# Two gate_up pieces of the first expert pair fetched outside the ring of weight slots

## The chip, the cores and the metric

One NeuronCore of one Trainium2 chip. The time is that of one execution on the device in microseconds, the median of three runs.

## The reference

One layer of a streaming encoder in float32. 272 prompt rows (16 meta tokens and 256 others) and 8 x 16 sample rows go through an RMS norm, an input projection, two kinds of attention (8 heads with a forget bias, 4 differential heads), an output projection and a residual. Then a mixture of 32 experts, four for each row, is added. The mixture's weights are what this case is about:

```python
D_MODEL = 1024; N_EXPERTS = 32; TOP_K = 4; D_FF = D_MODEL
SWIGLU_LIMIT = 7.0; SWIGLU_ALPHA = 1.702
...
def ffn(h, l):
    return h + _moe(_rms(h, ffn_norm[l]), w_router[l], b_router[l], w_gate_up[l], b_gate_up[l],
                    w_down[l], b_down[l])
```

Each expert has w_gate_up (1024 x 2048), a clamped SwiGLU, and w_down (1024 x 1024). Every expert is computed, so 32 x 12.6 MB of weights are read, 403 MB in all, whatever the routing is.

## The kernel before

All of SBUF is one tensor, `arena`, cut by hand into regions that stages share one after the other. Each engine has a program of its own, and semaphores order them. The attention half fills about the first 250 us. Then come the output projection in six steps (`project_out`, line 1752, each counted by `o_done` and added to `y` by VectorE), the router for three tiles of rows (`logits`, `route`; counted by `logit_done`, and by `gates_ready` when the last gates are written), and a first gather of rows (`gather_first`, line 1824).

The mixture runs over 16 **pairs** of experts. For each pair the host layout gives 12 **pieces** of 128 x 4096 float32 (2 MiB, one DMA each, issued by SP): pieces 0 to 7 are gate_up (two experts in turn, four quarters of 256 weight rows each), pieces 8 to 11 are down. Counted through all pairs they are pieces 0 to 191. They lie in a **ring** of 8 slots (`RING`); piece q stands in slot (q + 2) % 8. SP's `refill` waits until TensorE has finished piece j (`piece_done`) and then issues piece j + 8 into the same slot. TensorE's `pair` (line 1881 gate_up, line 1916 down) waits for two pieces at a time: pieces 0 and 1 at the pair's start, 2 and 3, 4 and 5, 6 and 7 at steps k = 2, 4, 6, then 8 and 9, 10 and 11. After a pair's gate_up it gathers the next pair's rows (line 1856), transposes the activations (1898), multiplies by down, and scatters the rows back (1931).

Pieces of the first pair can't be fetched as soon as their slots exist, since the slots hold attention data and output weights at first. Before the loop SP issues pieces 1, 3 and 2 (line 534), then, when attention is over, the router's weights and pieces 4 and 5 (line 538). Pieces 6 and 7 go to slots 0 and 1, where the output projection's weights lie until its last step: SP waits for `o_done` 6, issues six small bias loads (lines 541 and 543), then pieces 6 and 7 (line 545). Piece 8 waits for piece 0 to be done (line 553, in a hardware loop over pairs two at a time).

In the last pair TensorE runs some products into an unused bank (`keep_busy`, line 1742), which are idle filling.

Of the kernel before, what the change touches and what calls it, by code (L numbers as in the profile page):

```python
# [12 lines left out]
D = 1024  # L13
# [19 lines left out]
PAIRS = E // 2  # L33
# [3 lines left out]
SLOT_W = 2048  # L37
PIECE_W = 4096
LEAD = 2
Y_BASE = 6  # L40
X_ORDER = (1, 2, 3, 0)
X_BANK = (6, 2, 6, 0)
# [48 lines left out]
def build(nc, io, out):  # L91
    ctx = ExitStack()
    with ctx:
# [5 lines left out]
        def sem(name):  # L99
            return ctx.enter_context(nc.semaphore(name))  # L100

        def at(off, n):
            return arena[:, off:off + n]
# [92 lines left out]
        gT = at(a0 + 13312, 384)  # L196
        sel = [at3(a0 + 13696 + 768 * i, 3, P) for i in range(2)]
        selg = [at3(a0 + 13696 + 768 * i + 384, 3, P) for i in range(2)]
        rt = at(a0 + 11264, 512)
        EQ = [at3(a0 + 12288 + P * t, E, TOPK) for t in range(3)]  # L200
        EG = at3(a0 + 12288 + 3 * P, E, TOPK)
        bgu4 = at(hn0, 512)
# [12 lines left out]
        ovo = at(hn0 + 3008, 80)  # L215
        ovm = at(hn0 + 3088, 16)
        junk2 = act

        ident = C["ident"]

# [10 lines left out]
        s_x = [sem(f"s_x{t}") for t in range(4)]  # L231
        s_win = [sem(f"s_win{b}") for b in range(6)]
        s_wout = sem("s_wout")
        ring_in = [sem(f"ring_in{i}") for i in range(RING)]
        s_ck, s_cv = [sem("s_ck0"), sem("s_ck1")], [sem("s_cv0"), sem("s_cv1")]
        s_v3 = [sem("s_v3_0"), sem("s_v3_1")]
# [148 lines left out]

        block = ctx.enter_context(nc.Block())

        def run_pairs(eng, body):

            with eng.Fori(0, PAIRS // 2 - 1) as it:
                for u in range(2):
                    body(it, u, lambda k, c, u=u: it * (2 * k) + (u * k + c),
                         lambda k, c, u=u: it * (2 * k) + ((u + 1) * k + c))
            it = PAIRS // 2 - 1
            for u in range(2):
                body(it, u, lambda k, c, u=u: (2 * it + u) * k + c,
                     (lambda k, c, u=u: (2 * it + u + 1) * k + c) if u == 0 else None)
# [18 lines left out]
        def _(sp):  # L417
# [116 lines left out]
                sp.dma_start(piece_slot(s), piece_src(0, s - LEAD)).then_inc(ring_in[s], 16)  # L534
            sp.wait_ge(mixed, NA)
            sp.dma_start(w_rt, io["w_router"][0].rearrange("(k p) e -> p k e", p=P)).then_inc(s_wrt, 16)
            for n_ in (4, 5):
                sp.dma_start(piece_slot(n_ + LEAD), piece_src(0, n_)).then_inc(ring_in[n_ + LEAD], 16)
            sp.wait_ge(o_done, 6)
            for n in range(4):  # L540
                sp.dma_start(bgu4[E * n:E * (n + 1)], io["b_gate_up"][0, :, 512 * n:512 * (n + 1)]).then_inc(s_bgu, 16)
            for hf in range(2):
                sp.dma_start(bdn2[E * hf:E * (hf + 1)], io["b_down"][0, :, 512 * hf:512 * (hf + 1)]).then_inc(s_bdn, 16)
            for n_ in (6, 7):
                sp.dma_start(piece_slot(n_ + LEAD - RING), piece_src(0, n_)).then_inc(ring_in[n_ + LEAD - RING], 16)

            def refill(it, j):

# [3 lines left out]
                s = (q + LEAD) % RING  # L552
                sp.dma_start(piece_slot(s), piece_src(pair, q % PIECES)).then_inc(ring_in[s], 16)

            with sp.Fori(0, PAIRS // 2 - 1) as it:
                for j in range(2 * PIECES):
                    refill(it, j)
            for j in range(2 * PIECES - RING):
# [906 lines left out]
        def _(pe):  # L1465
# [378 lines left out]
            gather_first(1, (4, 5, 6, 7))  # L1844
            gather_first(2, range(8))
            totals()
            pe.wait_ge(s_bgu, 64)
            pe.wait_ge(s_bdn, 32)

            def gather(at_, u):
# [9 lines left out]
            def pair(at_, u, arrived, next_at=None, last_one=False):  # L1861
                steps = [(k, n) for k in range(6) for n in range(4)] + [(k, n) for n in range(4) for k in (6, 7)]
                for k, n in steps:
                    if (k, n) == (0, 0):
                        pe.wait_ge(xg_a, at_(4, 1))
                    if (k, n) == (1, 0):
                        pe.wait_ge(own_ready, at_(1, 1))
                        for n_ in range(4):
                            grp = slice(E * n_, E * (n_ + 1))
                            mm(banks[n_], own_e[u][grp], bgu4[grp], start=False, stop=False, skip_group_check=True)  # L1870
                        pe.wait_ge(xg_a, at_(4, 4))
                    if (k, n) == (4, 0):
                        pe.wait_ge(xg_v, at_(1, 1))
                    if (k, n) == (6, 0) and last_one:
                        keep_busy(banks[7], 512, 2)
                    if k % 2 == 0 and n == 0:
                        s = [arrived(k + x) for x in range(2)]
                    for x in range(2):
                        half = slice(SLOTS * x, SLOTS * (x + 1))
                        c0 = 2 * FF * (k % 2) + 512 * n  # L1880
                        last = mm(banks[n][half], XT[u][:, k, half], piece_slot(s[x])[:, c0:c0 + 512],  # L1881
                                  start=(k == 0), stop=(k == 7), skip_group_check=True)
                        if n == 3 and k % 2 == 1:
                            last.then_inc(piece_done, 1)
                    if n < 3 and k == 7:
                        last.then_inc(h_done, 1)
                if next_at:
                    gather(next_at, 1 - u)
                pe.wait_ge(act_ready, at_(4, 2))
                for hf in range(2):  # L1890
                    grp = slice(E * hf, E * (hf + 1))
                    mm(banks[hf], own_e[u][grp], bdn2[grp], start=True, stop=False, skip_group_check=True)  # L1892
                if last_one:
                    keep_busy(banks[7], 512)
                pe.wait_ge(y_added, at_(6, Y_BASE))
                pe.wait_ge(act_ready, at_(4, 4))
                for c in range(8):
                    last = nc.tensor.transpose(banks[4 + c // 4][:, P * (c % 4):P * (c % 4 + 1)],  # L1898
                                               act[:, P * c:P * (c + 1)], ident)
                    if c % 4 == 3:  # L1900
                        last.then_inc(actT_done, 1)
                pe.wait_ge(selg_ready, at_(1, 1))
                for t in range(3):
                    last = nc.tensor.transpose(banks[3][:, P * t:P * (t + 1)], selg[u][:, t], ident)
                last.then_inc(selT_done, 1)
                pe.wait_ge(actT_a, at_(1, 1))
                for i in range(2):
                    if i == 1:
                        pe.wait_ge(actT_v, at_(1, 1))
                    s = [arrived(8 + 2 * i + x) for x in range(2)]  # L1910
                    for hf in range(2):
                        for c in range(4):
                            for x in range(2):
                                half = slice(SLOTS * x, SLOTS * (x + 1))
                                w = piece_slot(s[x])[:, D * c + 512 * hf:D * c + 512 * (hf + 1)]
                                last = mm(banks[hf][half], actT[:, 4 * i + c, half], w, start=False,  # L1916
                                          stop=(i == 1 and c == 3), skip_group_check=True)
                                if c == 3 and hf == 1:
                                    last.then_inc(piece_done, 1)
                        if i == 1 and hf == 0:  # L1920
                            last.then_inc(down_done, 1)
                pe.wait_ge(selT_copied, at_(1, 1))
                for n in range(6):
                    t, hf = n // 2, n % 2
                    if n == 0:
                        pe.wait_ge(rows_a, at_(1, 1))
                    elif n == 1:
                        pe.wait_ge(rows_v, at_(1, 1))
                    else:
                        pe.wait_ge(y_added, at_(6, Y_BASE + n - 1))  # L1930
                    mm(banks[4 + n % 2], gT[:, P * t:P * (t + 1)], rows[:, 512 * hf:512 * hf + 512],  # L1931
                       start=True, stop=True).then_inc(scat_done, 1)

            def main(it, u, at_, nx):
                def arrived(r):
                    q = PIECES * u + r
                    s = (q + LEAD) % RING
                    pe.wait_ge(ring_in[s], it * (16 * 3) + 16 * (q // RING + 1))
                    return s
                pair(at_, u, arrived, nx, nx is None)  # L1940

            run_pairs(pe, main)

            def over(p, r_, at_):
                def arrived(r):
                    s, uses, use = over_slot(r)
                    before_ = 16 * PAIRS * PIECES // RING
                    pe.wait_ge(ring_in[s], at_(16 * uses, before_ + 16 * (use + 1) - PAIRS * 16 * uses))
                    return s
                pe.wait_ge(y_added, at_(6, Y_BASE))  # L1950
                gather(at_, 0)
                pair(at_, 0, arrived)
# [33 lines left out]
```

## Time and profile before

| | us |
|---|---|
| median of 3 runs | 1246.28 (1246.19 to 1246.39) |
| the profiled execution, whole | 1244.19 |
| its span in the trace | 1242.40 |
| TensorE matmul busy | 1211.3 (97%) |
| TensorE weight loads busy | 530.0 (43%) |
| VectorE, ScalarE, GpSimd busy | 349.7, 194.6, 158.6 |
| DMA: 448.59 MB moved | mean 361 GB/s |

Matmul busy time overlaps itself and counts pipelining, so it is not a distance from the peak. The page's second part cuts the span into 40 slices of 31 us; a digit 9 is a share of 90% or more. Times below are counted from the span's start.

### The profile page before, as it was taken

The page shows a single profiled execution, that of the slowest core. Times are in us where ns is not written, and L with a number is a line of the kernel's source. Part 1 is how long each engine was busy: PE and PEld are TensorE (multiplying, and loading weights), DVE is VectorE, ACT ScalarE, POOL GpSimd, SP SyncE. Part 2 cuts the span into 40 slices and gives each one's busy share as a digit, 9 for nine tenths or more (in the row PEclk, how much of TensorE's full clock was granted, in tenths as well). Part 3 has the DMA queues.
Part 4 walks back from the last instruction along what each step waited for, and adds up shares of the span by engine and source line. Part 5 has one row for each costly group of instructions (what it writes and reads, how often), then busy time and mean ns, then how long its engine had stood idle before and what let it go on. Part 6 is the DMA issues. An engine that isn't in the chain of part 4 may idle for free.

```text
span 1242.4 us, 16212 instructions
## 1 busy us (share of the span) xinstructions
PE 1211.3 (97%) x6099; PEld 530.0 (43%) x6100; DVE 349.7 (28%) x929; ACT 194.6 (16%) x519; POOL 158.6 (13%) x378
## 2 busy tenths in 40 slices
PE   9999999999999999999999999999999999999997
PEld 5444456646344343434343443434343434243432
DVE  3234366613322121213131322212121212131312
ACT  4211365513101010101010100001010101010100
POOL 0032312101320202112020202020202011020000
PEclk9999999999999999999999999999999999999999
DMA  9622344792899999999999999999999999999994
GB/s 299 256 71 93 146 131 148 276 394 72 367 428 428 428 429 427 428 429 429 427 428 429 429 427 427 429 430 428 428 428 429 429 427 428 429 429 427 427 427 198
DMA packets 55450, 448.59 MB, mean 361 GB/s; under 512 B 10465, under 2 KB 11890, under 8 KB 30834
## 3 DMA queue, kind: packets, MB, share of 16 engines
q1 hardware_dynamic: 55368, 448.05, 87.1%
q8 instruction: 25, 0.41, 0.1%
q14 instruction: 15, 0.12, 0.0%
q10 hardware_dynamic: 42, 0.01, 0.0%
HBM read 442.00 MB, written 4.86 MB: 360 GB/s over the span
## 4 chain that ended last, share of the span: by engine, by line
PE 71%; DMA 25%; DVE 1%; issue 1%; SPq 1%; ACT 0%; POOL 0%; DVEq 0%; POOLq 0%
DMA arena<-in_w_gate_up 23%; PE psum L1881 18%; PE psum L1916 17%; PE psum L1627 10%; PE psum L1856 7%; PE psum L1752 3%; PE psum L1931 3%; DMA arena<-in_w_down 2%; PE psum L1892 1%; PE psum L1898 1%; PE psum L1663 1%; PE psum L1731 1%; PE psum L1586 1%; PE psum L1577 1%; PE psum L1602 1%
## 5 line engine op out<-in xcount | busy, mean ns | idle before, releaser
L1881 PE MATMUL psum<-arena 128*64 128x512 f32 x2048 | 454.0, 600 | 15.8 <-DMA arena<-in_w_gate_up 15.8
L1881 PEld LDWEIGHTS psum<-arena 128*64 128x64 f32 x2048 | 148.8, 138 | 316.2 <-issue 316.2
L1916 PE MATMUL psum<-arena 128*64 128x512 f32 x1024 | 223.5, 594 | 0.9
L1426 DVE TENSOR_SCALAR arena<-psum 128x256 f32<-128x256 f32 x64 | 26.8, 419 | 397.3 <-PE psum L1881 397.3
L1916 PEld LDWEIGHTS psum<-arena 128*64 128x64 f32 x1024 | 78.7, 137 | 134.8 <-issue 133.3
L1627 PE MATMUL psum<-arena 128*128 128x512 f32 x288 | 127.3, 596 | 1.4 <-DVE arena L1065 1.4
L1002 ACT ACTIVATE arena<-arena 128x256 f32<-128x256 f32 x64 | 26.7, 418 | 594.8 <-DVE arena L1426 594.8
L1931 PE MATMUL psum<-arena 128*128 128x512 f32 x192 | 93.2, 622 | 0.0
L700 POOL COPY arena<-arena 128x6 f32 (+1 forms) x16 | 3.0, 188 | 698.2 <-PE psum L1916 695.1
L1856 PEld LDWEIGHTS psum<-arena 128*128 128x128 f32 x720 | 81.5, 192 | 12.2 <-issue 12.2
L1856 PE MATMUL psum<-arena 128*128 128x128 f32 x720 | 84.4, 277 | 0.0
L1627 PEld LDWEIGHTS psum<-arena 128*128 128x128 f32 x288 | 53.5, 190 | 64.4 <-issue 62.4
L1444 DVE TENSOR_TENSOR arena<-psum,arena 128x512 f32<-128x512 f32 x96 | 66.4, 692 | 25.3 <-PE psum L1931 25.3
L1439 DVE COPY arena<-psum 128x512 f32<-128x512 f32 x16 | 11.1, 692 | 218.3 <-PE psum L1916 218.3
L1931 PEld LDWEIGHTS psum<-arena 128*128 128x128 f32 x192 | 28.6, 188 | 64.3 <-DVE arena L1444 42.1
L717 POOL TENSOR_SCALAR arena<-arena 128x64 f32<-128x64 f32 x96 | 53.9, 579 | 0.0
L1752 PE MATMUL psum<-arena 128*128 128x512 f32 x96 | 43.1, 597 | 1.0 <-DVE arena L1313 1.0
L1414 DVE TENSOR_TENSOR arena<-arena 128x256 f32<-128x256 f32 x64 | 36.4, 610 | 5.4
L708 POOL TENSOR_SCALAR arena<-arena 128x64 f32<-128x64 f32 x90 | 37.4, 441 | 0.0
L1010 ACT ACTIVATE arena<-psum 128x512 f32<-128x512 f32 x16 | 9.6, 598 | 161.1 <-PE psum L1916 161.1
L1399 DVE TENSOR_SCALAR arena<-psum,arena 128x128 f32<-128x128 f32 x64 | 18.0, 345 | 48.1 <-PE psum L1856 45.8
L1428 DVE SCALAR_TENSOR_TENSOR arena<-arena 128x256 f32<-128x256 f32 x64 | 27.3, 426 | 2.2
(257 smaller groups left out, 795.0 us busy)
## 6 DMA issues: line engine op xcount, KB each, us to landing
arena<-in_w_gate_up SPq DMA_DIRECT2D x128, 2048.0 KB, 25.0
arena<-in_w_down SPq DMA_DIRECT2D x64, 2048.0 KB, 22.1
arena<-in_w_in SPq DMA_DIRECT2D x5, 2048.0 KB, 14.1
arena<-in_cache_fox_k SPq DMA_DIRECT2D x8, 512.0 KB, 3.6
arena<-in_cache_diff_k SPq DMA_DIRECT2D x8, 512.0 KB, 4.5
arena<-in_cache_fox_v SPq DMA_DIRECT2D x8, 512.0 KB, 4.7
arena<-in_cache_diff_v SPq DMA_DIRECT2D x8, 512.0 KB, 5.8
arena<-in_w_out SPq DMA_DIRECT2D x4, 1024.0 KB, 6.7
```

Of the source, the lines that this page charges most:

```text
L708: last = nc.gpsimd.tensor_scalar(sel[u][:, t, cols], places, pRK[u][:, t, x:x + 1], None, ALU.is_equal)
L717: last = nc.gpsimd.tensor_scalar(selg[u][:, t, cols], places, pRK[u][:, t, x:x + 1], pG[u][:, t, x:x + 1], ALU.is_equal, ALU.mult)
L1414: nc.vector.tensor_tensor(act_rows[:, 32 * n:32 * (n + 1)], ta[n % 2].rearrange("s (p q) -> s p q", q=8), sg[n % 2].rearrange("s (p q) -> ...
L1426: nc.vector.tensor_scalar(tg[n % 2], H[:, 0:512:2], 7.0, None, ALU.min).then_inc(glu_ready, 1)
L1428: lk(nc.vector.scalar_tensor_tensor(out=ta[n % 2], in0=tl[n % 2], scalar=1.0, in1=tg[n % 2], op0=ALU.add, op1=ALU.mult))
L1444: nc.vector.tensor_tensor(y[:, t, cols], banks[4 + n % 2], y[:, t, cols], ALU.add).then_inc(y_added, 1)
L1627: last = mm(z_bank(u), hnT[:, k, r0:r0 + n], wv[:, k], start=(k == 0), stop=(k == 7))
L1752: last = mm(banks[4 + n % 2], oT[:, k, P * t:P * (t + 1)], wv[:, k % 2, 512 * hf:512 * hf + 512], start=(k == 0), stop=(k == 7))
L1856: last = mm(banks[6 + k // 4][:, P * (k % 4):P * (k % 4 + 1)], x2n[:, t, P * k:P * (k + 1)], sel[u][:, t], start=(t == 0), stop=(t == 2))
L1881: last = mm(banks[n][half], XT[u][:, k, half], piece_slot(s[x])[:, c0:c0 + 512], start=(k == 0), stop=(k == 7), skip_group_check=True)
L1916: last = mm(banks[hf][half], actT[:, 4 * i + c, half], w, start=False, stop=(i == 1 and c == 3), skip_group_check=True)
L1931: mm(banks[4 + n % 2], gT[:, P * t:P * (t + 1)], rows[:, 512 * hf:512 * hf + 512], start=True, stop=True).then_inc(scat_done, 1)
```

## The change

Pieces 4 and 5 of the first pair leave the ring. Their ring slots (6 and 7) are filled at once with pieces 0 and 1 of the second pair (pieces 12 and 13). Piece 5 goes whole into the region of the activation buffers (`whole_piece`), once the second tile's logits and the last square are done. Piece 4 goes in four runs of columns (1024, 1024, 1280 and 768) into regions that are dead after the routing, once the third tile's logits, the first gather and the gates are done. The loads before the loop are put in another order: piece 6 right after `o_done` 6, then the gate_up biases, piece 5, piece 7, the down biases, piece 4. TensorE waits for the biases where it uses them. On TensorE the first two pairs are written out ahead of the hardware loop, and piece 4's product is cut where a run ends inside a block of 512 columns. SP leaves out the two refills. A small routing buffer (`rt`) moves.

```diff
+APART = (4, 5)
+APART_SLOTS = [(q + LEAD) % RING for q in APART]
...
-        rt = at(a0 + 11264, 512)
+        rt = at(a0 + 12800, 512)
...
+        whole_piece = at(a0 + 8192, PIECE_W)
+        runs = [(0, a0 + 7168, 1024), (1024, a0 + 12288, 1024), (2048, hn0 + 1024, 1280), (3328, a0 + 13312, 768)]
...
+        def run_pairs(eng, body, first_apart=False):
+            if first_apart:
+                for u in range(2):
+                    body(0, u, lambda k, c, u=u: u * k + c, lambda k, c, u=u: (u + 1) * k + c)
+            with eng.Fori(1 if first_apart else 0, PAIRS // 2 - 1) as it:
...
-            for n_ in (4, 5):
-                sp.dma_start(piece_slot(n_ + LEAD), piece_src(0, n_)).then_inc(ring_in[n_ + LEAD], 16)
+            for q, s in zip(APART, APART_SLOTS):
+                sp.dma_start(piece_slot(s), piece_src(1, q + RING - PIECES)).then_inc(ring_in[s], 16)
             sp.wait_ge(o_done, 6)
+            sp.dma_start(piece_slot(6 + LEAD - RING), piece_src(0, 6)).then_inc(ring_in[6 + LEAD - RING], 16)
             for n in range(4):
                 sp.dma_start(bgu4[E * n:E * (n + 1)], io["b_gate_up"][0, :, 512 * n:512 * (n + 1)]).then_inc(s_bgu, 16)
+            sp.wait_ge(logit_done, 2)
+            sp.wait_ge(h_sq, 4)
+            sp.dma_start(whole_piece, piece_src(0, APART[1])).then_inc(s_apart[1], 16)
+            sp.dma_start(piece_slot(7 + LEAD - RING), piece_src(0, 7)).then_inc(ring_in[7 + LEAD - RING], 16)
             for hf in range(2):
                 sp.dma_start(bdn2[E * hf:E * (hf + 1)], io["b_down"][0, :, 512 * hf:512 * (hf + 1)]).then_inc(s_bdn, 16)
-            for n_ in (6, 7):
-                sp.dma_start(piece_slot(n_ + LEAD - RING), piece_src(0, n_)).then_inc(ring_in[n_ + LEAD - RING], 16)
+            sp.wait_ge(logit_done, 3)
+            sp.wait_ge(xg_done, 2)
+            sp.wait_ge(gates_ready, 1)
+            for p0, where, n in runs:
+                sp.dma_start(at(where, n), piece_src(0, APART[0])[:, p0:p0 + n]).then_inc(s_apart[0], 16)
...
-            with sp.Fori(0, PAIRS // 2 - 1) as it:
+            for j in range(2 * PIECES):
+                if j not in APART:
+                    refill(0, j)
+            with sp.Fori(1, PAIRS // 2 - 1) as it:
...
-            pe.wait_ge(s_bgu, 64)
-            pe.wait_ge(s_bdn, 32)
...
+                        pe.wait_ge(s_bgu, 64)
...
-                        last = mm(banks[n][half], XT[u][:, k, half], piece_slot(s[x])[:, c0:c0 + 512],
-                                  start=(k == 0), stop=(k == 7), skip_group_check=True)
+                        for o, w in s[x](c0):
+                            last = mm(banks[n][half, o:o + w.shape[1]], XT[u][:, k, half], w,
+                                      start=(k == 0), stop=(k == 7), skip_group_check=True)
...
+                pe.wait_ge(s_bdn, 32)
...
+                    if isinstance(it, int) and it == 0 and q in APART:
+                        i = APART.index(q)
+                        pe.wait_ge(s_apart[i], 16 * (len(runs), 1)[i])
+                        return (run_parts, piece_parts(whole_piece))[i]
+                    pe.wait_ge(ring_in[s], it * (16 * 3) + (16 * (q // RING + 1) - fewer(s)))
...
-            run_pairs(pe, main)
+            run_pairs(pe, main, first_apart=True)
```

## Rows read from the trace of the kernel before

**Rows 1.** The page, parts 1 and 2: TensorE's busy time; DMA share in 40 slices.

```profile
PE 1211.3 (97%) x6099; PEld 530.0 (43%) x6100; DVE 349.7 (28%) x929; ACT 194.6 (16%) x519; POOL 158.6 (13%) x378
...
DMA  9622344792899999999999999999999999999994
```

**Rows 2.** Waits of TensorE, whole run: total us, times, longest.

```profile
PE psum L1881 <- DMA arena<-in_w_gate_up: 15.8, 10, 2.1
```

**Rows 3.** Windows, second and eighth pair: us, engines' busy time, PE clock, DMA share, GB/s.

```profile
367.30:423.80 56.50, 56.50 (x278) 22.57 (x277) 13.30 (x28) 5.78 (x12) 6.74 (x17) 1.00 1.01 429
...
734.20:792.90 58.70, 56.68 (x275) 22.84 (x275) 13.31 (x28) 5.79 (x12) 6.75 (x17) 1.00 1.01 429
```

**Rows 4.** The chain that ended last, in order of time: start, us, what.

```profile
315.44 24.18 PE psum L1881 x112
...
675.49 8.75 PE psum L1881 x32
...
734.22 7.09 PE psum L1881 x32
...
1197.23 26.34 DMA arena<-in_w_down
1223.57 0.14 issue
1223.71 7.09 PE psum L1916 x32
```

**Rows 5.** DMA issues near 305.0, 319.2, 326.6, 332.9, 375.8 us: last column, us to landing.

```profile
arena<-in_w_gate_up SPq DMA_DIRECT2D x1, 2048.0 KB, 8.0
...
arena<-in_w_down SPq DMA_DIRECT2D x1, 2048.0 KB, 7.2
...
arena<-in_w_down SPq DMA_DIRECT2D x1, 2048.0 KB, 14.5
...
arena<-in_w_gate_up SPq DMA_DIRECT2D x1, 2048.0 KB, 14.6
...
arena<-in_w_down SPq DMA_DIRECT2D x1, 2048.0 KB, 10.7
```

**Rows 6.** Timeline of SP's queue: start, us for all issues of the row, line, count.

```profile
302.30 1.72 SPq L541 DMA_DIRECT2D arena<-in_b_gate_up  x4
...
304.98 0.90 SPq L545 DMA_DIRECT2D arena<-in_w_gate_up  x2
319.22 0.99 SPq L553 DMA_DIRECT2D arena<-in_w_down  x2
...
332.94 0.33 SPq L553 DMA_DIRECT2D arena<-in_w_gate_up  x1
...
375.79 0.91 SPq L553 DMA_DIRECT2D arena<-in_w_down  x2
```

**Rows 7.** Windows before and in the first pair; the last two columns are DMA's.

```profile
290.00:300.00 10.00, 10.00 (x45) 5.95 (x43) 4.77 (x19) 3.65 (x8) 0.00 (x0) 1.00 0.01 2
...
317.00:318.00 1.00, 1.00 (x7) 0.29 (x5) 0.00 (x0) 0.00 (x0) 0.91 (x5) 1.00 0.00 0
```

**Rows 8.** DMA queues, stretches 345:346, 320:424, then 424:1120 (two rows): packets, MB, share.

```profile
q8 instruction: 1, 0.02, 6.6%
...
q8 instruction: 3, 0.05, 0.2%
...
q1 hardware_dynamic: 20478, 298.26, 100.7%
q14 instruction: 1, 0.01, 0.0%
```

**Rows 9.** Timeline before and in the first pair: last gather, last gate copy.

```profile
307.62 3.02 PE L1824 MATMUL psum<-arena 128*128 128x128 f32 x24
...
312.89 0.15 DVE L1449 COPY arena<-arena 128x1 f32<-128x1 f32 x1
```

**Rows 10.** Window inside the 8.75 us stretch of the chain; PE clock before the DMA columns.

```profile
675.50:678.80 3.30, 3.30 (x8) 1.08 (x10) 0.00 (x0) 0.00 (x0) 0.00 (x0) 0.50 1.04 442
```

More of the change, by code:

```diff
@@ L217, in build, with run_parts, piece_parts @@
         junk2 = act
+        whole_piece = at(a0 + 8192, PIECE_W)
+        runs = [(0, a0 + 7168, 1024), (1024, a0 + 12288, 1024), (2048, hn0 + 1024, 1280), (3328, a0 + 13312, 768)]
+        def run_parts(c0):
+            return [(max(p0, c0) - c0, at(where + max(p0, c0) - p0, min(p0 + n, c0 + 512) - max(p0, c0)))
+                    for p0, where, n in runs if p0 < c0 + 512 and p0 + n > c0]
+        def piece_parts(piece):
+            return lambda c0: [(0, piece[:, c0:c0 + 512])]
         ident = C["ident"]
@@ L233, in build @@
         s_wout = sem("s_wout")
+        s_apart = [sem("s_apart0"), sem("s_apart1")]
         ring_in = [sem(f"ring_in{i}") for i in range(RING)]
@@ L386, in build, with fewer @@
         block = ctx.enter_context(nc.Block())
-        def run_pairs(eng, body):
-            with eng.Fori(0, PAIRS // 2 - 1) as it:
+        def fewer(s):
+            return 16 if s in APART_SLOTS else 0
+        def run_pairs(eng, body, first_apart=False):
[3 more added lines that the diff above has]
+            with eng.Fori(1 if first_apart else 0, PAIRS // 2 - 1) as it:
                 for u in range(2):
@@ L1914, in pair @@
                                 half = slice(SLOTS * x, SLOTS * (x + 1))
-                                w = piece_slot(s[x])[:, D * c + 512 * hf:D * c + 512 * (hf + 1)]
+                                w = s[x](D * c + 512 * hf)[0][1]
                                 last = mm(banks[hf][half], actT[:, 4 * i + c, half], w, start=False,
@@ L1937, in arrived @@
                     s = (q + LEAD) % RING
-                    pe.wait_ge(ring_in[s], it * (16 * 3) + 16 * (q // RING + 1))
-                    return s
+                    if isinstance(it, int) and it == 0 and q in APART:
[3 more added lines that the diff above has]
+                    pe.wait_ge(ring_in[s], it * (16 * 3) + (16 * (q // RING + 1) - fewer(s)))
+                    return piece_parts(piece_slot(s))
                 pair(at_, u, arrived, nx, nx is None)
-            run_pairs(pe, main)
+            run_pairs(pe, main, first_apart=True)
             def over(p, r_, at_):
@@ L1947, in arrived @@
                     before_ = 16 * PAIRS * PIECES // RING
-                    pe.wait_ge(ring_in[s], at_(16 * uses, before_ + 16 * (use + 1) - PAIRS * 16 * uses))
-                    return s
+                    pe.wait_ge(ring_in[s], at_(16 * uses, before_ + 16 * (use + 1) - fewer(s) - PAIRS * 16 * uses))
+                    return piece_parts(piece_slot(s))
                 pe.wait_ge(y_added, at_(6, Y_BASE))
```

## The prediction

> **What bounds the kernel now.** I read the page first: TensorE shows 97%, and from the tenth slice on the DMA digits are 9 to the end [rows 1]. Two resources are nearly full, so the question is which is late at each place. The waits of TensorE answer for the whole run: in the mixture it waits for weights ten times, 15.8 us in all [rows 2]. The windows by pair say when. The second pair takes 56.5 us with TensorE never idle, the eighth 58.7 us with the same matmuls; the DMA share is full and its rate 429 GB/s in both [rows 3]. So a pair costs TensorE 56.5 us and DMA 58.7 us, that is 58.7 / 12 = 4.89 us a piece. TensorE starts with a store of filled slots, loses 2.2 us of it in each pair, and from the sixth or seventh pair on DMA sets the pace. The chain agrees: the last piece lands at 1197.23 + 26.34 = 1223.57, and 0.14 us later TensorE does its last half of down [rows 4]. The end is therefore the time at which DMA last had nothing to do, plus 4.89 us for each piece left, plus a tail that the change leaves alone.
>
> Where did DMA last stand idle? Issues and landings tell. Piece 8 is issued at 319.22 [rows 6] and lands 7.2 us later [rows 5], at 326.4: 4.9 us of moving and 2.3 us of start and receipt. DMA moved nothing from 317 to 319 [rows 7]. Piece 20, issued at 375.79, lands 10.7 us later, at 386.5; it queued. From there 171 pieces follow to 1223.57, 4.895 us each: no gap at all.
>
> **The change part by part.** (a) *Less to move later.* Two pieces, 9.8 us of DMA, go ahead of the first pair's refills. It can be had only while DMA would be idle. Before 302 it is idle (rate 2 GB/s [rows 7]), but no new slot opens there: slots 6 and 7 are filled at the same place as before, with pieces 12 and 13 for 4 and 5. What is new is that piece 6 is issued at 302.30, where the biases were, for 304.98 [rows 6] (2.7 us), and that pieces 5, 7 and 4 fill the hole before 319.22.
>
> (b) *The ring gives most of it back.* A ring of eight can't hold more than TensorE has released. Piece 20 needs the slot of piece 12, and TensorE finishes piece 12 at 375.79 [rows 6] however early the weights came. Following the queue at 4.9 us a piece: 6 lands at 302.30 + 7.2 = 309.5; the gate_up biases (256 KB at 429 GB/s) 0.6; piece 5 at 315.0, 7 at 319.9, the down biases 0.3, 4 at 325.1; then 8, 9, 10, 11, 14 and 15 at 354.5. Now DMA is out of work: piece 16 is issued when piece 8 is done, about 354.9, and lands at 362; 19 at 377; piece 20 at 375.79 + 7.2 = 383.0, for 386.5 before. **The gain at piece 20 is 3.5 us, not 9.8.** At the same place of the next pair the queue is ahead of nothing: 383.0 + 12 x 4.89 = 441.7 against an issue at 375.79 + 56.5 = 432.3, so DMA never idles again and the 3.5 us last, but for (c).
>
> (c) *A lag that comes back.* Landings are 4.9 us apart but for one step: piece 11, issued near 326.6, lands at 341.1, and piece 12, issued at 332.94, at 347.5 [rows 5, 6]. That is 6.4 us, 1.5 too many. In it stands one instruction fetch of 16 KB, 6.6% of 16 engine-microseconds, so 1.06 us of one engine [rows 8]. A piece has landed when its slowest engine has, so one such hit on a full queue costs 1.5 us for good; later hits cost nothing (three fetches lie in 320 to 424, and the step occurs once), presumably because other engines have that much in hand. An empty queue wipes the lag out. In the new kernel the queue runs empty before piece 20, so the next fetch on the full queue brings the 1.5 us back: the gain falls to 2.0 us. The fetches come from TensorE's code: none in the loop from 424 to 1120, where one q14 packet is the only other one in 20,479 [rows 8]. With two pairs written out there will be four or five more, and I charge them nothing, since extra hits were free; a second hit on the lagging engine would cost 1.5 us more.
>
> The Trainium skill (DMA: Bandwidth & Descriptors, Queues, rings and completion order) says that each DMA engine takes its queues in turn, packet by packet; that speaks against more fetched code on a full queue, and the one step of 1.5 us agrees with it. The skill (Advanced Engine Details and Errata, ISA Cache) also gives TensorE 128 KB of instruction cache in lines of 16 KB; by it the loop body still fits, and no run here shows that yet.
>
> (d) *TensorE waits in the first pair.* Step k = 4 needs pieces 4 and 5. It begins 48 of 112 instructions into the stretch from 315.44: 315.44 + 48 x 0.216 = 325.8 [rows 4]. Piece 4 lands at 325.1 if nothing disturbs the queue; a fetch like that of (c) in this stretch, now full, makes it 326.6, and TensorE goes on 0.14 us later [rows 4]: a stall of 0.9 us. That stall moves every release after it, that of piece 12 too, so it comes off the gain in full. Between 0 and 0.9 I take 0.9, since TensorE's code is fetched all along these pairs (three times from 320 to 424 [rows 8]). Piece 4 is issued after the gates, 312.89 + 0.15 = 313.0 (the gather ends before, 310.6) [rows 9]; the queue before it is busy to 320.2, which hides the wait by 7 us. Its shorter rows (3 to 5 KB for 16) and four starts have no row; in a full queue I take 0, bounded from above in the rivals. Behind this wait of SP stand the refills, the first due at 319.22: SP is through at 313.0 + 4 x 0.43 = 314.8.
>
> (e) *Small things.* The gate_up biases land at 310.1 for a use at 314.4, the down biases at 320.2 for one at 345: hidden behind matmuls by 4 and 25 us. One block of 512 columns is cut in two: at most 0.1 us of TensorE. SP leaves out two issues and waits the same.
>
> Sum on the profiled execution: -3.5 + 1.5 + 0.9 = **-1.1 us**, 1244.19 to 1243.1. The median of the runs is 2.09 above the profiled one, so 1246.28 - 1.1 = **1245.2 us**.
>
> Dips of the clock don't enter: after the wait that ends at 675.49 the same 32 instructions take 8.75 us for 7.09 [rows 4], since in the stretch behind it the granted clock is 0.50, the level of 1.2 GHz [rows 10]; but in the part that DMA paces the next wait is shorter by as much.
>
> **The rivals.**
> *No lag, no stall in the first pair* (the fetch falls on an engine that has time): -2.0, 1244.3.
> *The lag doesn't come back*: the full 3.5 us, 1242.8, or 1243.7 with the stall. For it: many fetches cost nothing. Against: before, the first one on a full queue did cost.
> *The ring is no limit* and 9.8 us arrive: 1236.5. Against it stands the release of piece 12 at 375.79.
> *A second lag*, from the extra code or on the engine already late: +1.5 on the forecast, 1246.7. A clock dip in the first or second pair, after the new stall, would cost 8.75 - 7.09 = 1.7 and give 1246.9; waits of 2.1 us came before such a dip [rows 2, 4], mine is shorter.
> *Slower: piece 4's four DMAs each pay a start.* A lone piece needs 2.3 us beyond its moving [rows 5]. If three more starts of 2.3 stood one after the other, piece 4 would land at 333.5, the stall would be 7.8 us, and the sum -3.5 + 1.5 + 7.8 = +5.8: 1252.1. It decides from a stall of 2.0 us on (same time), and from 4.5 on it is slower by over 0.2%. Against it: pieces that queue behind one another land 4.9 us apart, with no start between them [rows 5].
>
> **How the numbers follow.** About 0.2%, 2.5 us, is what a measurement of this kernel can tell from no change. Forecast (lag and stall) 0.48; no stall 0.22; second lag or dip 0.10; lag doesn't come back 0.12 (two thirds of it faster by over 0.2%); ring no limit 0.02; slower 0.06. Faster: 0.08 + 0.02 and some for a start that comes cheaper than 7.2, 0.12. Slower: 0.06. Within: 0.82. The range from 1243.3 to 1246.8 takes in the forecast, no stall and the second lag, and leaves out the full gain and the slow case, under 2 in 10.
>
> **What would show it.** Right: DMA busy from 303 to about 354 with no hole; a gap of 1 to 2 us before pieces 16 and 20; piece 20 issued at 375.8 to 376.8 and landed near 383 to 384; a step of 6.4 us between two landings after that; a wait of TensorE of about 1 us near 326; total waits of TensorE for weights about 1 us smaller or equal. Wrong: a landing of the last piece more than 3 us earlier (then the ring was no limit, or the lag no law), a wait near 326 over 2 us (then the four runs are dear), or instruction fetches inside the hardware loop.

## The result and the profile after

| | before | changed kernel |
|---|---|---|
| median, us (20 runs each) | 1244.52 | 1248.26 |
| lowest and highest | 1243.18 to 1248.49 | 1245.29 to 1250.37 |
| the profiled execution, whole | 1244.19 | 1245.48 |
| its span | 1242.40 | 1243.7 |

The ratio is 1.0022 (95% interval 1.0014 to 1.0029): the change makes the kernel slower by 2.7 us (the medians differ by 3.7), where 1.1 us faster was forecast. The two profiled executions differ by only 1.3 us; 12 of the 20 runs of the changed kernel stand at 1248 or more, and of before 1 in 20. So there are two things to find: 1.3 us between the two profiles, and something that only some runs have.

The waits of TensorE in the changed kernel (total us, times, longest):

```profile
PE psum L1911 <- DMA arena<-in_w_gate_up: 15.2, 11, 2.1
PE psum L1911 <- issue: 2.0, 1, 2.0
PE psum L1947 <- DMA arena<-in_w_down: 1.6, 1, 1.6
```

The first line answers [rows 2] and is 0.6 us smaller. The second is new, in the first pair. The third is the wait for the last piece, which comes later than before. The chain that ended last shows where the second is, and how the kernel ends (start, us, what):

```profile
310.67 3.58 PE psum L1911 x16
314.25 1.07 PE psum L1899 x8
315.32 10.45 PE psum L1911 x48
325.78 2.03 issue
327.81 13.99 PE psum L1911 x64
...
369.41 3.58 PE psum L1911 x16
...
1195.56 29.18 DMA arena<-in_w_down
...
1224.88 7.09 PE psum L1947 x32
```

The wait of 2.03 us is at step k = 4 of the first pair, as expected at 325.8, but more than twice as long. The profile names no releaser for it ("issue"). The DMA issues do: the last of piece 4's four runs, issued at 314.36, lands 13.4 us later, at 327.7, and TensorE goes on at 327.81. The second pair then begins at 369.41. The last piece lands at 1195.56 + 29.18 = 1224.74, 1.17 us after that of before [rows 4]; so the loss of the profiled run is at its DMA end.

SP's queue (start, us for all issues of the row) and the landings of single issues (near 302.2, 304.6, 305.0, 314.4, 318.9, 377.7: pieces 6, 5, 7, the last run of 4, 8 and 20; last column us to landing):

```profile
302.18 0.33 SPq L559 DMA_DIRECT2D arena<-in_w_gate_up  x1
302.55 1.91 SPq L561 DMA_DIRECT2D arena<-in_b_gate_up  x4
304.56 0.37 SPq L564 DMA_DIRECT2D arena<-in_w_gate_up  x1
304.97 0.46 SPq L565 DMA_DIRECT2D arena<-in_w_gate_up  x1
...
313.02 1.77 SPq L572 DMA_DIRECT2D arena<-in_w_gate_up  x4
318.93 7.67 SPq L580 DMA_DIRECT2D arena<-in_w_down  x4
...
377.68 7.67 SPq L580 DMA_DIRECT2D arena<-in_w_down  x4
```

```profile
arena<-in_w_gate_up SPq DMA_DIRECT2D x1, 2048.0 KB, 8.8
...
arena<-in_w_gate_up SPq DMA_DIRECT2D x1, 2048.0 KB, 12.2
...
arena<-in_w_gate_up SPq DMA_DIRECT2D x1, 2048.0 KB, 17.2
...
arena<-in_w_gate_up SPq DMA_DIRECT2D x1, 384.0 KB, 13.4
...
arena<-in_w_down SPq DMA_DIRECT2D x1, 2048.0 KB, 13.7
...
arena<-in_w_down SPq DMA_DIRECT2D x1, 2048.0 KB, 7.4
```

Piece 20 is issued 1.9 us later than before (375.79 [rows 6]) and still lands at 377.68 + 7.4 = 385.1, 1.4 us earlier than its 386.5 [rows 5, 6], because the queue ahead of it is nearly empty (piece 19 lands at 380.1). The hole in DMA is filled, too: 393 GB/s from 317 to 318, where before nothing moved [rows 7]:

```profile
317.00:318.00 1.00, 1.00 (x8) 0.41 (x6) 0.00 (x0) 0.00 (x0) 0.92 (x4) 1.00 0.92 393
```

From 1.4 us early at piece 20 to 1.17 us late at the end, 2.6 us are lost on a queue that is full all the time. One part is the lag forecast in (c): two landings at 399.7 and 405.8, 6.0 us apart where 4.9 is the rule, so 1.15 us. Another is new. Issues near 1152.8 and near 1167.4, two neighbours in the ring (pieces 183 and 184):

```profile
arena<-in_w_gate_up SPq DMA_DIRECT2D x1, 2048.0 KB, 31.6
...
arena<-in_w_gate_up SPq DMA_DIRECT2D x1, 2048.0 KB, 23.2
```

They land at 1184.4 and, unrounded, 1190.66, 6.3 us apart: a second lag of 1.4 us. Up to there the changed kernel is level with before (1223.57 - 8 x 4.895 = 1184.4 for the same piece).

### The profile page after: what moved, and what is told of

Same layout as the page of the kernel before. It is cut to its first block, busy times and chain, and to the rows that moved or that the text cites. A ratio compares the mean times of both kernels' runs of the same rounds, so it can differ in the third digit from the quotient of the medians.

```text
span 1243.7 us, 16154 instructions
## 1 busy us (share of the span) xinstructions
PE 1209.2 (97%) x6101; PEld 529.9 (43%) x6102; DVE 349.6 (28%) x929; ACT 194.9 (16%) x519; POOL 158.9 (13%) x378
## 4 chain that ended last, share of the span: by engine, by line
PE 73%; DMA 23%; DVE 1%; issue 1%; ACT 0%; SPq 0%; POOL 0%; ACTq 0%; DVEq 0%; POOLq 0%
DMA arena<-in_w_gate_up 21%; PE psum L1911 20%; PE psum L1947 17%; PE psum L1657 10%; PE psum L1884 7%; PE psum L1782 3%; PE psum L1962 3%; DMA arena<-in_w_down 2%; PE psum L1923 1%; PE psum L1929 1%; PE psum L1761 1%; PE psum L1693 1%; PE psum L1616 1%; PE psum L1899 1%; PE psum L1723 1%
## 5 line engine op out<-in xcount | busy, mean ns | idle before, releaser
L1911 PEld LDWEIGHTS psum<-arena 128*64 128x64 f32 x2050 | 150.5, 138 | 314.6 <-issue 314.4
```

The source lines that it names most:

```text
L1911: last = mm(banks[n][half, o:o + w.shape[1]], XT[u][:, k, half], w, start=(k == 0), stop=(k == 7), skip_group_check=True)
```

## The experiments

Each ratio is against runs of the kernel before on the same chip in the same session.

**Written-out code alone.**

```diff
-            run_pairs(pe, main)
+            run_pairs(pe, main, written_out=True)
```

with `run_pairs` as in the change and nothing else of it.

> The kernel before, with TensorE's first two pairs written out ahead of its loop and nothing else changed. Theory A (the ring and the stall): extra instruction fetches fall on DMA engines that have time in hand, so the time is that of before within 0.3 us, last piece landed near 1223.6; one second lag would make it +1.4. Theory B (code): the four or five extra fetches are what makes the changed kernel slow, so this one alone is +1.3 us in its fastest runs and has the group of runs 4 to 5 us above. Theory C (an idle TensorE at step 4 of the first pair brings a clock dip in some runs): no stall here, so no such group.

Measured: 1246.13 against 1245.92, ratio 1.0007 (0.9998 to 1.0016). Lowest run 1244.92, against 1243.41. In its profile the first step is where it was before; a second one stands late. Issues near 1109 and near 1115.2:

```profile
arena<-in_w_gate_up SPq DMA_DIRECT2D x1, 2048.0 KB, 26.0
...
arena<-in_w_gate_up SPq DMA_DIRECT2D x1, 2048.0 KB, 26.2
```

1134.9 and 1141.3: 6.4 us apart. So the code alone brings a second lag. The time by itself is unclear at this size: its interval holds 1, and it also holds the 1.4 us (1.0011) that the lag would cost. The step in the trace is clear.

**Four pairs written out**, the loop from the fifth on (`Fori(2, ...)`), otherwise as before.

> The kernel before with TensorE's first four pairs written out (some ten fetches more than before). Fetch rule (eight engines in turn): the first step of 1.5 us comes near 345, the second at the eighth fetch after it, near 550 to 580, already in the written-out part, and a third one at the sixteenth if the fetches reach so far; the last piece lands 1.4 to 2.9 us after 1223.6. If the second step hangs on the end of the kernel and not on the count of fetches, it stays near 1140.

Measured: 1247.61 against 1244.11, ratio 1.0020 (1.0010 to 1.0030). Now the second step stands in the middle. Issues near 527.0 and 533.3:

```profile
arena<-in_w_gate_up SPq DMA_DIRECT2D x1, 2048.0 KB, 23.5
...
arena<-in_w_gate_up SPq DMA_DIRECT2D x1, 2048.0 KB, 23.7
```

550.5 and 557.0, 6.5 us apart. It moved from 1140 to 557 with the count of fetches, not with the end of the kernel. The time, 2.5 us over before, is more than the 1.6 us of one such step, but its interval begins at 1.2 us. Counted in the traces, the second step comes with the eighth 16 KB fetch after the one that made the first. The DMA queues between the two, first in the changed kernel (401.5 to 1190), then written-out code (346 to 1139.7), then four pairs (349 to 555.9), then the kernel before to its last landings (346.5 to 1220):

```profile
q8 instruction: 8, 0.13, 0.1%
```

```profile
q8 instruction: 8, 0.13, 0.1%
```

```profile
q8 instruction: 8, 0.13, 0.3%
```

```profile
q8 instruction: 6, 0.10, 0.0%
```

Eight, eight, eight; and before, where no second step occurs, only six. The same count holds in all eleven profiles that have a second step, those of the experiments below among them. In two of these (piece 5 alone, and the fourth further profile of the changed kernel) the first step comes one fetch earlier, at 372.6 and 373.8 instead of near 400, and the second is one fetch earlier too, at 1159.7 and 1162.3. The six profiles without a second step have fewer than eight such fetches before the last landing. The steps aren't all equal: the second is 0.9 to 1.6 us long. Fetches seem to go round eight DMA engines: seven in a row find an engine with time in hand, the eighth meets the late one again. Which engine a fetch ran on the trace doesn't show, so the round of eight is a reading of the counts. The third step that a sixteenth fetch would bring could not be seen, since the sixteenth came after the last landing.

**Piece 4 before piece 7.**

```diff
-            sp.dma_start(piece_slot(7 + LEAD - RING), piece_src(0, 7)).then_inc(ring_in[7 + LEAD - RING], 16)
...
             for p0, where, n in runs:
                 sp.dma_start(at(where, n), piece_src(0, APART[0])[:, p0:p0 + n]).then_inc(s_apart[0], 16)
+            sp.dma_start(piece_slot(7 + LEAD - RING), piece_src(0, 7)).then_inc(ring_in[7 + LEAD - RING], 16)
```

> The changed kernel, with the four runs of piece 4 issued before piece 7. Piece 4 then lands near 322.5, piece 7 near 327.7 for a use at 333: no stall in the first pair. Theory A: 2.0 us under before (0.6 with a second lag), as with piece 5 alone. Theory B: 1 us or more above before. Theory C: no group of slow runs.

Measured: 1244.06 against 1245.92, ratio 0.9993 (0.9984 to 1.0002). No wait in the first pair; in the chain the 112 matmuls stand in one piece:

```profile
314.94 24.25 PE psum L1911 x112
```

The slot of piece 12 is free in time again, and piece 20 is issued and lands (near 375.1):

```profile
375.07 0.80 SPq L580 DMA_DIRECT2D arena<-in_w_down  x2
```

```profile
arena<-in_w_down SPq DMA_DIRECT2D x1, 2048.0 KB, 7.4
```

375.07 + 7.4 = 382.5, near the 383.0 of the prediction. It keeps the second lag, and its last piece lands at 1192.85 + 29.04 = 1221.89:

```profile
1192.85 29.04 DMA arena<-in_w_down
```

That is 2.85 us before the changed kernel's, from one line in another place: 2.0 us are the wait, 0.4 a mixture that began earlier in this run, and both steps are smaller here too (5.9 and 5.8 us between landings).

**Piece 5 alone apart**: `APART = (5,)`, piece 4 in the ring, its four DMAs and their waits gone.

> The changed kernel with piece 5 alone fetched apart; piece 4 stays in the ring, and the first pair has nothing to wait for late. Theory A: the ring's release of piece 12 at 375.8 sets the gain, one piece fills the hole as well as two, and without the stall of 2.0 us piece 20 lands at 383.0 for 386.5 before; less 1.4 us of lag that comes back, the time is 2.0 us under before, or 0.6 under it with a second lag late. Theory B: same code as the changed kernel, so still 1 us or more above before. Theory C: no stall, so no group of slow runs.

Measured: 1244.20 against 1245.92, ratio 0.9994 (0.9984 to 1.0004), last landing at 1193.38 + 29.48 = 1222.86. One piece brings what two bring.

```profile
1193.38 29.48 DMA arena<-in_w_down
```

**No more code than before.** On top of piece 4 before piece 7, TensorE's pairs are laid out as pair 0, a loop over pairs 1 to 14, pair 15:

```diff
-            run_pairs(pe, main, first_apart=True)
+            main(0, 0, lambda k, c: c, lambda k, c: k + c)
+            with pe.Fori(1, PAIRS // 2) as it:
+                main(it, 1, lambda k, c: it * (2 * k) + (c - k), lambda k, c: it * (2 * k) + c, 1)
+                main(it, 0, lambda k, c: it * (2 * k) + c, lambda k, c: it * (2 * k) + (k + c))
+            main(PAIRS // 2 - 1, 1, lambda k, c: (PAIRS - 1) * k + c, None)
```

The last argument 1 takes 48 from the ring's wait, since the pair belongs to the round before. The kernel ran twice.

> Piece 4 issued before piece 7, and TensorE's pairs laid out as pair 0, a loop over pairs 1 to 14 two at a time, pair 15: no more code than before (two pairs outside the loop, two in it). Fetch rule: if instruction fetches go round eight DMA engines, so that the eighth fetch after the first one on a full queue hits the lagging engine again, then with five fetches fewer that eighth one is gone; no second step near 1140 to 1190, the last piece lands near 1220.5, and the fastest runs are 1.4 us below those of the kernel with written-out pairs, some 2.5 us under before. If the second step is not the extra code's, it stays, and the time is that of the written-out kernel, within 0.5 us.

> Piece 4 before piece 7, both apart, and TensorE's pairs laid out as pair 0, a loop over pairs 1 to 14, pair 15 (the kernel of the run same_code, unaltered). Ring and lag theory: 1.5 to 2.5 us under before, as there. If the first result was chance, the interval of the ratio covers 1.

Measured: 1242.41 against 1244.11, ratio 0.9988 (0.9979 to 0.9997), and 1243.26 against 1244.18, ratio 0.9988 (0.9979 to 0.9997). Both times faster than before, by 1.5 us at that ratio; of the fastest runs 2.5 had been expected, and 1241.33 is 2.1 below 1243.41. The last piece lands at 1221.4 in the first profile (expected near 1220.5). No late step in either profile. In the first one DMA isn't even last at the end: the last down stands in one piece of 13.99 us, with no wait for its weights.

```profile
1214.59 13.99 PE psum L1947 x64
```

**The same loop with piece 5 alone apart.**

> The same loop, with piece 5 alone apart and piece 4 in the ring. Ring theory: the release of piece 12's slot near 375.5 sets the gain, one piece fills DMA's idle time as well as two, and the time is that of the kernel with two pieces apart within 0.5 us. If the gain went with the bytes fetched early, half of it (1 us) would be missing here.

Measured: 1242.93 against 1244.18, ratio 0.9987 (0.9977 to 0.9997). The second piece apart adds nothing that these intervals can show.

**The changed kernel with that loop** (piece 4 last, the wait kept).

> The changed kernel as it is (piece 4 last, so with its stall of 2 us in the first pair), with only TensorE's pairs laid out as pair 0, a loop, pair 15, so no more code than before. Fetch rule: the second step of 1.4 us near 1190 is gone and the last piece lands 1.4 us earlier than in the changed kernel: near 1223.3, level with before; time within 0.5 us of before. If the stall alone makes the changed kernel slow, it is still 1 us or more above before.

Measured: 1245.47 against 1244.18, ratio 1.0011 (1.0002 to 1.0020). The step near 1190 is gone, as expected, and by the ratios half of the loss (the intervals of 1.0011 and 1.0022 overlap, so that half is rough). "Within 0.5 us of before" was missed: it is 1.4 us above. So was the last landing, expected near 1223.3: it comes at 1224.48, only 0.3 us before the changed kernel's. What differs in the trace is the first step. Here a fetch starts at 373.9, and piece 20 lands 9.8 us after its issue (near 377.8) instead of 7.4; the fetch near 400 then costs nothing. This one hit costs about what the two steps cost the changed kernel, so its profile alone doesn't show the gain. The pair with piece 4 before piece 7 does: counted from the first matmul of the mixture, the last landing comes 1.2 us earlier without the written-out code (910.5 against 911.7). The wait of 1.81 us is there:

```profile
arena<-in_w_down SPq DMA_DIRECT2D x1, 2048.0 KB, 9.8
```

```profile
326.10 1.81 issue
```

**The order of the loads alone**: before, with pieces 6 and 7 issued as in the change and the waits for the biases moved, nothing apart.

> The kernel before with only the loads ahead of the loop in the new order (piece 6, biases, piece 7, biases) and TensorE's waits for the biases where it uses them; nothing is fetched apart. Ring theory: pieces 6 and 7 land 2 us earlier and nobody waits for them, piece 8 is still issued when piece 0 is done, near 319: no change, within 0.3 us. If the earlier start itself brought part of the gain, this would be up to 2 us faster.

Measured: 1244.40 against 1244.18, ratio 1.0005 (0.9995 to 1.0015). No change that can be told, as the ring demands: piece 8 waits for piece 0. The last piece lands at 1223.58 in its profile, for 1223.57 before.

**A filled wait.** Two products (four matmuls in the profile, 2.0 us) into an unused bank ahead of step 4 of the first pair:

```diff
+                    if (k, n) == (4, 0) and first:
+                        for _ in range(2):
+                            mm(banks[7], ident, x2n[:, 0, 0:512], start=True, stop=True, skip_group_check=True)
```

> The changed kernel with four matmuls of 128x512 into an unused bank (2.0 us) ahead of step 4 of the first pair, where TensorE stands idle for 2.0 us. The stall in time is the same, only TensorE is not idle in it. If the idle time brings a clock dip in some runs, the group of runs at 1248 to 1250 is gone and all are near 1245.5. If the group is still there, the idle time isn't its cause.

**The changed kernel again**, beside it.

> The changed kernel once more, unaltered, beside the others on one chip. Its runs fall into a group near 1245.5 and one at 1248 to 1250. If its profile is of the upper group, a dip of the clock in the first two pairs shows in it: TensorE's stretch of 112 matmuls takes 25.9 us for 24.2, piece 20 is issued later by 1.7 us. If the upper group has another cause, the profile shows no dip there.

Measured: filled 1246.57 against 1244.11, ratio 1.0023 (1.0014 to 1.0032), 2 of 11 runs at 1248 or more; the changed kernel 1247.04, ratio 1.0019 (1.0008 to 1.0030), also 2 of 11. By what was expected, a group of upper runs that stays speaks against idle time as its cause. But in the filled kernel's profile the wait was 2.8 us long, and TensorE still stood idle for 0.9 us of it, so the filling was too short to decide.

**Four more profiles of the changed kernel**, to find an upper run among them.

> The changed kernel unaltered, one more profile. Longer wait: in an upper run the wait at step 4 is 3 us or more, and piece 20 is issued later by as much. Clock dip: the wait is 2.0 us as before, and a stretch at 0.50 lies between 310 and 420 us. Late loss: neither, and the last pairs differ.

> The changed kernel unaltered, one more profile; the same expectations as for the first look: longer wait at step 4 (3 us or more), or a stretch at clock 0.50 between 310 and 420 us, or a difference in the last pairs.

> The changed kernel unaltered, one more profile; the same expectations as for the first look: longer wait at step 4 (3 us or more), or a stretch at clock 0.50 between 310 and 420 us, or a difference in the last pairs.

> The changed kernel unaltered, one more profile; the same expectations as for the first look: longer wait at step 4 (3 us or more), or a stretch at clock 0.50 between 310 and 420 us, or a difference in the last pairs.

Measured: 1250.05, 1246.75, 1246.75, 1246.63. The first is an upper run. Two windows of it (PE clock is the third number from the right), and its chain:

```profile
252.40:255.70 3.30, 3.30 (x19) 1.37 (x12) 0.00 (x0) 0.37 (x2) 1.11 (x3) 0.50 1.08 453
330.90:334.20 3.30, 3.30 (x10) 1.14 (x8) 0.00 (x0) 0.00 (x0) 0.00 (x0) 0.50 1.02 432
```

```profile
312.78 3.58 PE psum L1911 x16
...
327.89 2.35 issue
330.23 15.68 PE psum L1911 x64
...
1201.22 27.51 DMA arena<-in_w_down
```

Two dips to 1.2 GHz, both where TensorE sets the pace. One is before the mixture, whose first matmul comes at 312.78 and not at 310.67: 2.1 us. The other begins 0.6 us after the wait at step 4 ends, and the 64 matmuls behind it take 15.68 us for 13.99: 1.7 us. With the longer wait (2.35 for 2.03) these make 4.1 us, and the last piece lands at 1228.73, 4.0 us after the profiled run's 1224.74. The second profile has only the earlier dip, the third and fourth neither. Their waits at step 4, first to fourth:

```profile
PE psum L1911 <- issue: 2.3, 1, 2.3
```

```profile
PE psum L1911 <- issue: 1.6, 1, 1.6
```

```profile
PE psum L1911 <- issue: 2.3, 1, 2.3
```

```profile
PE psum L1911 <- issue: 2.5, 1, 2.5
```

So the wait lasts 1.6 to 2.5 us, and in one profile of six a dip follows it. The earlier dip isn't peculiar to the changed kernel: the profiles of four pairs written out, of piece 5 alone with the other loop and of the second run of no more code each have a dip near 10 us, and their mixture begins at 313.0 to 313.2.

Do the counts of runs fit a dip after the wait? In part. The kernels with the wait (changed, changed again, filled, changed with the other loop) have 18 of 54 runs at 1248 or more, and those without it (piece 4 first, piece 5 alone, the other loop with either) 0 of 55. But the second group is faster throughout, so one line for both counts too much. Reckoned from each kernel's own fastest run (of before, the fastest of each session), 11 of 54 lie 4 us or more above it with the wait, 2 of 55 without, and 2 of the 115 runs of before; at 3 us it is 19, 8 and 21. The far upper runs do go with the wait. That a clock dip makes them was seen once, and by my estimate an earlier dip together with a wait of 2.5 us would reach 1248 as well (1245.48 + 2.1 + 0.5); their cause stays open.

## Why the prediction was wrong

*What bounds the kernel* held: the end is DMA's end, and the gains and losses were read off the landings. In two of the profiles with the other loop (the first of no more code, and the changed kernel with it) the last down runs without a wait, so TensorE comes last there by some tenths of a microsecond.

*(a) and (b), the ring.* Held. Without a wait piece 20 lands at 382.5 (383.0 forecast), not 9.8 us early. One piece apart does what two do (0.9987 and 0.9988), and the new order alone does nothing that can be told (1.0005). The release of piece 12 sets the gain.

*(c) A lag that comes back*: held, at 1.15 us for 1.5. The profiled run is 1.4 us ahead at piece 20 and level at piece 183. **"I charge them nothing" failed.** [Rows 8] has two fetches after the first step that cost nothing, and I carried that on to seven and more; the eighth costs 1.4 us here. The prediction had this as a rival (a second lag, +1.5, with the clock dip at a chance of 0.10). Five more fetches brought it in all six profiles of the changed kernel, in that of the written-out code alone, and in the two variants that keep that code. The trace agrees with a loop body that fits, since it isn't fetched again in these 600 us; one profile, that of the new order alone, has a single fetch inside its loop, at 652.4. Eight lines are also as many as the fetches from step to step, so the round may be one of lines and not of DMA engines; no run here tells the two apart.

*(d) The wait in the first pair*: right place, wrong size: **0.9 us forecast, 2.03 measured**, 1.6 to 2.5 in the other profiles. The term that failed is the queue's progress up to piece 4. Undisturbed, pieces 5, 7 and 4 were to land at 315.0, 319.9 and 325.1; they landed at 316.8, 322.1 and 327.7, so 1.8, 2.2 and 2.6 us late. One lag of 1.5 us was allowed for, and 1.1 us come beyond it. Most is lost before piece 5 has landed, and not all of that to a fetch of code. In the changed kernel with the other loop no 16 KB fetch lies between 300 and 319.6; piece 6 is issued at 302.5, and piece 5, issued at 304.8, lands 11.7 us later, at 316.5. From the one to the other these are 14.0 us, where the forecast has 12.7. Between the two stand the four gate_up biases, priced by their bytes at 0.6 us. [Rows 5] already had 8.0 us for the piece behind such small loads, where I took the 7.2 of a lone one. That the small loads are so dear isn't shown by a run of its own, so the cause of that part stays open.

```profile
arena<-in_w_gate_up SPq DMA_DIRECT2D x1, 2048.0 KB, 11.7
```

The four DMAs with short rows cost 0.3 us: piece 4 lands 5.6 us after piece 7, and with piece 5 alone apart, piece 8 lands in its place 5.3 after. The slow rival (three more starts, a wait of 7.8 us) is refuted, and so is the sign by which a wait over 2 us would mean that the four runs are dear.

*The sum* with measured terms: -3.5 + 1.15 + 2.0 + 1.4 = +1.05 us (-3.5 is 382.5 for 386.5 less the 0.5 us by which that run's mixture began earlier, 310.29 for 310.79); the last piece lands 1.17 later, and the profiled execution is 1.3 longer.

*The base.* The forecast's 1246.28 was the median of three runs that lay high; 20 runs have 1244.52. From there the same sum gives 1243.4, so the base hid part of the miss.

*Dips of the clock* I counted as absorbed. That holds only where DMA sets the pace. The dip seen after the wait in the first pair cost 1.7 us in full, because every release of a slot was late by it. The rival was named and priced at 1.7 us, its chance set low because the wait was taken to be 0.9 us. It may be what takes the ratio (2.7 us) beyond the profiled difference (1.3); with one such run seen in a profile, that isn't shown.

Where the loss of 2.7 us sits, by ratios: the wait with what follows it 2.3 per mille (1.0011 against 0.9988, same loop, piece 4 moved), the extra code 0.5 to 1.1 per mille (0.9993 against 0.9988; 1.0022 and 1.0019 against 1.0011). Each of these is a comparison of two intervals of about 0.9 per mille half-width, so the parts are rough; the steps and waits in the traces carry them.

## What to carry to other kernels

Fetching early helps a ring that is refilled on release only up to a point: look for the first refill that starts at once on its release, and price everything up to it at nothing. An early fetch that is itself late costs its whole wait, because the wait delays the releases that bound the gain. Put the transfer with the earliest use first even if it can be issued last. And keep straight-line copies of a loop body out of a DMA-bound kernel: here two pairs written out added five fetches of code, and with them a second step of 1.4 us in the stream of weights.

## What the runs showed of the hardware

A 16 KB instruction fetch on a full DMA queue delayed the next landings by 0.7 to 1.6 us in most profiles (1.5 in before, 1.15 in the changed kernel), though it takes one engine about 1.06 us [rows 8]. In three profiles it came while the queue ran nearly empty, and piece 20 landed 9.0 to 9.8 us after its issue instead of 7.4. No trace shows the loss made good on a full queue. The next seven fetches cost nothing that shows, and the eighth costs 0.9 to 1.6 us again (steps that end at 1190.7, 1141.3 and 557.0 in three kernels, eight fetches after the first step in each of eleven profiles). And a TensorE wait of 2.35 us was followed by a stretch at the lower of the two clock levels in one run, and waits of 2.5, 2.3 and 2.0 us were not in others.
